# Low parts of two weight chunks in one VectorE operation, in the plain steps of the first w_down stage

## What is computed

```python
h = rms_norm(x, norm_ffn_g[i])
u = causal_dwconv(h @ w_up[i], ffn_conv_w[i])
u_g, u_v = jnp.split(u, 2, axis=-1)
x = x + (jax.nn.silu(u_g) * u_v) @ w_down[i]        # w_down: 5632 x 2048, float32
```

## Time and profile before

| | |
|---|---|
| median of 3 runs | 1567.11 us (1565.79 to 1567.94) |
| the profiled execution, its own time | 1566.66 us |
| its span in the trace | 1564.9 us |
| TensorE (PE) busy | 1558.2 us |
| VectorE (DVE) busy | 1097.1 us |
| ScalarE (ACT) busy | 792.3 us |
| granted clock of TensorE | 1.0 of full speed in all of the stage's windows |

### The profile page before, as it was taken

The page is one execution under the profiler, slowest core; times in us unless marked ns, Lnnn a source line. Parts: engine busy times, 40 slices in busy tenths (PEclk is TensorE's granted clock), DMA queues, the critical chain, the costliest instruction groups (busy, mean ns, idle before and its releaser), DMA issues.

```text
span 1564.9 us, 20899 instructions
## 1 busy us (share of the span) xinstructions
PE 1558.2 (100%) x7694; PEld 1316.9 (84%) x7694; DVE 1097.1 (70%) x1311; ACT 792.3 (51%) x944; POOL 33.7 (2%) x52
## 2 busy tenths in 40 slices
PE   9999999999999999999999999999999999999998
PEld 7878888888888888888888888888888888888887
DVE  6599867766676556555687777789867777755554
ACT  6355454444554544455455555545545555555443
POOL 5000110000000000000000000000000000000000
PEclk9999999999999999999999999999999999999999
DMA  8756665666655666666666566666766666666664
GB/s 260 207 174 189 198 174 168 196 183 188 201 180 174 198 200 195 188 182 180 188 184 194 176 184 203 188 185 204 217 187 187 189 188 175 199 201 188 187 189 149
DMA packets 157479, 297.35 MB, mean 190 GB/s; under 512 B 9655, under 2 KB 14499, under 8 KB 157408
## 3 DMA queue, kind: packets, MB, share of 16 engines
q1 hardware_dynamic: 156896, 296.13, 62.6%
q0 software_dynamic: 480, 0.26, 0.1%
q10 hardware_dynamic: 32, 0.01, 0.0%
HBM read 294.27 MB, written 2.10 MB: 189 GB/s over the span
## 4 chain that ended last, share of the span: by engine, by line
PE 97%; DVE 1%; ACT 0%; DMA 0%; issue 0%; SPq 0%; ACTq 0%
PE psum L541 21%; PE psum L568 18%; PE psum L570 18%; PE psum L569 18%; PE psum L547 11%; PE psum L530 2%; PE psum L532 2%; PE psum L531 2%; PE psum L747 0%; PE psum L693 0%; DVE w_lo L1380 0%; DMA xtok<-in_x 0%; PE psum L668 0%; PE psum L656 0%; PE psum L659 0%
## 5 line engine op out<-in xcount | busy, mean ns | idle before, releaser
L1380 DVE TENSOR_TENSOR w_lo<-raw,w_hi 128x1024 fp32r<-128x1024 f32 x547 | 664.4, 1222 | 379.0 <-ACT w_hi L1019 378.0
L1019 ACT CAST w_hi<-raw 128x1024 fp32r<-128x1024 f32 x546 | 569.7, 1049 | 585.9 <-PE psum L570 391.3
L541 PE MATMUL psum<-h_both,w_hi 128*128 128x512 f32 x1408 | 336.4, 391 | 0.0
L568 PE MATMUL psum<-w_hi,h_both 128*128 128x512 f32 x844 | 331.9, 393 | 0.0
L570 PE MATMUL psum<-w_hi,h_both 128*128 128x512 f32 x844 | 328.7, 389 | 0.0
L569 PE MATMUL psum<-w_lo,h_both 128*128 128x512 f32 x844 | 328.5, 389 | 0.0
L541 PEld LDWEIGHTS psum<-h_both,w_hi 128*128 128x128 f32 x1408 | 258.7, 188 | 50.4 <-DVE rB L1761 0.3
L570 PEld LDWEIGHTS psum<-w_hi,h_both 128*128 128x128 f32 x844 | 158.4, 188 | 33.3
L547 PEld LDWEIGHTS psum<-h_both,w_lo 128*128 128x128 f32 x1408 | 180.6, 191 | 6.9
L568 PEld LDWEIGHTS psum<-w_hi,h_both 128*128 128x128 f32 x844 | 158.5, 188 | 32.7 <-issue 0.3
L569 PEld LDWEIGHTS psum<-w_lo,h_both 128*128 128x128 f32 x844 | 158.6, 188 | 31.8
(11 more groups left out here) (326 smaller groups left out, 1399.0 us busy)
## 6 DMA issues: line engine op xcount, KB each, us to landing
raw<-in_w_up SPq DMA_DIRECT2D x176, 512.0 KB, 3.8
raw<-in_w_gate SPq DMA_DIRECT2D x96, 512.0 KB, 3.6
raw<-in_w_in SPq DMA_DIRECT2D x89, 512.0 KB, 3.7
raw<-in_w_down SPq DMA_DIRECT2D x88, 512.0 KB, 4.3
raw<-in_w_out SPq DMA_DIRECT2D x32, 512.0 KB, 4.1
raw<-in_w_ple_gate SPq DMA_DIRECT2D x32, 512.0 KB, 4.5
raw<-in_w_moba_out SPq DMA_DIRECT2D x16, 512.0 KB, 4.7
raw<-in_w_conv_out SPq DMA_DIRECT2D x8, 512.0 KB, 3.9
```

What stands on the lines that cost most here:

```text
L541: mm = nc.tensor.matmul(wide[part][:, j, :], w_hi[:, c % RING, w], h_both[:, kt + k, :, :].rearrange("p h s -> p (h s)"), start=first and ...
L568: nc.tensor.matmul(o, sh, w_hi[:, c % RING, w], start=first and k == 0, stop=False, skip_group_check=True)
L1019: A.copy(w_hi[:, c % RING, :], raw[:, c % RING, :]).then_inc(chunk_high, 1)
L1380: V.tensor_tensor(w_lo[:, c % RING, :], raw[:, c % RING, :], w_hi[:, c % RING, :].bitcast(F32), ALU.subtract).then_inc(chunk_split, 1)
```

## The change

In a plain step of the first w_down stage the low parts of both chunks are made by one operation over both slots (2 x 1024 columns), once the second chunk's high part is there. It adds 2 to `chunk_split`. Nothing is done any more at the step's first chunk. Chunks of the seven steps and all other stages keep `split`.

```diff
+        def split_pair(c):
+
+            splits[0] = c + 2
+            slots = slice(c % RING, c % RING + 2)
+            dve.wait_ge(chunk_high, c + 2)
+            V.tensor_tensor(w_lo[:, slots, :], raw[:, slots, :], w_hi[:, slots, :].bitcast(F32),
+                            ALU.subtract).then_inc(chunk_split, 2)
...
             g, s, side = place(k)
             c = DOWN1 + k
-            if g > 1 or s not in SEVENS[g]:
+            if g > 1:
                 split(c)
+                return
+            if s not in SEVENS[g]:
+                if side:
+                    split_pair(c - 1)
                 return
```

## The result

| | before | changed |
|---|---|---|
| median of 18 runs each | 1566.57 us | 1569.29 us |
| span of the profiled execution | 1564.9 us | 1567.7 us |
| TensorE busy | 1558.2 us | 1558.3 us |
| VectorE busy | 1097.1 us | 1096.7 us |

The ratio is 1.0018, with a 95% interval of 1.0011 to 1.0024: slower by 2.8 us, between 1.7 and 3.8. The three runs known ahead of the prediction had a median of 1567.11, the 18 have 1566.57.

The account below looks back on a forecast made before the run. TensorE was taken to bound the kernel, through its waits on VectorE. Losses of 1.12 + 1.80 + 0.28 less 0.76 us gave 2.44, hence a median of 1569.6 us, 0.16% slower, counted as the same; range 1566.7 to 1572.2.

Parts of the forecast that it names:

- What bounds the kernel: Whole kernel: TensorE, busy 1558.2 of 1564.9 us, so time moves only with its waits; two old waits cost 0.76 us.
- The operation: VectorE's joint operation of 2048 columns: 2.29 us taken, saving about 1 us over 16 pairs.
- Chunks 0 to 3: First two pairs of the stage: no cost to TensorE, but the scaling of `upv` moves by 1.06 us.
- Chunks 4 and 5: Pair behind VectorE's first tap, delayed through the late scaling: TensorE loses 1.12 us.
- Chunks 6 and 7: Pair behind `full`, with its cast about 1 us late: TensorE loses 1.80 us.
- Chunks 8 and 9: Seven step: VectorE 2.06 us late, TensorE later still, so both old waits go, saving 0.76 us.
- Chunks 10 and 11: Pair behind the first seven step, its casts late: TensorE loses 0.28 us.
- The sum: Whole stage: losses at chunks 4, 6 and 10 less the old waits, 2.44 us slower; given 65%.
- Behind that: From pair 14, 15 on: no further wait, by a margin of 0.45 us, the cycle repeating with later steps.
- Late loads: Rival: later issued loads delay the seven steps' sums, slower by over 0.2%, 1570.3 to 1572.5 us; 21%.
- Nothing is lost: Rival: TensorE finds the pairs ready and old waits shrink, -0.8 to +0.5 us, 1566.3 to 1567.6; 14%.

Follow-up runs that it names:

- the expectation for chunks 12 and up: Joint operations only for chunks 12 and up, single ones before, against the changed kernel; expected -0.2 to +0.3 us, measured stage time 126.43 us, +0.55 against before, ratio 1.0000.
- the kernel with two operations: Changed kernel with the joint operation split into two of 1024 columns, both issued at the step's second chunk; stage time 125.94 us, +0.06 against before, ratio 1.0001.

## Why the prediction was right

*What bounds the kernel.* TensorE's waits alone carried the difference: its busy time is the same within 0.1 us, the sum of its lost time is 2.74 of 2.78 us.

*The operation.* 2.29 us was taken, 2.28 to 2.29 measured for all 16. The saving of about 1 us of VectorE's busy time came out as 0.4; the sum didn't use it.

*Chunks 0 to 3.* The pair 2, 3 was to cost TensorE nothing and to make the scaling 1.06 us late. Measured: no wait there, and the scaling 1.14 later against chunk 0's first matmul (1010.44 - 1006.71 against the end of the old operation at 1009.23 plus 0.03, less 1006.67). The kernel with this pair alone shows that link: +1.13 us.

*Chunks 4 and 5.* Expected 1.12 us lost, measured 1.22. *Chunks 6 and 7.* Expected 1.80, measured 1.94. *Chunks 8 and 9.* No wait expected, none seen; `t_lo` ended at 1034.03, and the first matmul behind its wait started at 1034.37 without idle time. *Chunks 10 and 11.* Expected 0.28, measured 0.34. The sum, 2.44, was 0.3 too small. Much of that is a few hundredths at each link: the joint operation starts 0.10 us behind its cast and not 0.03, and `full` 0.10 behind the second tap's end and not 0.03. That the median of 1569.29 lies within 0.3 us of the 1569.6 foretold is in part luck: the starting value, the median of three runs, was 0.54 too high and the sum 0.3 too low. The change itself, 2.7 to 2.8 us against 2.44, is the fairer comparison.

*Behind that.* No further wait was expected, by a margin of 0.45 at chunk 14, and none was seen. The margin was 0.28: the pair 14, 15 ended at 1046.49, with the 0.2 for coming into step that is 1046.69, and TensorE started chunk 14 at 1046.97. The sums for chunk 12 came 2.49 us later than before, and not 2.06, with their load the last that they waited for. The prediction had written down where this rests, TensorE's own delay. In the expectation for chunks 12 and up I left it out, and missed that waits can come when that delay isn't there.

*Late loads.* This rival is refuted for the changed kernel: its rounds between sums are 1047.10 - 1037.11 = 9.99 and 9.87 us, against 10.25 before and 10.05 in the next round, which the prediction didn't look at, and VectorE's idle time ahead of the sums is 0.49 to 0.61 us, not longer than the 0.60 and 1.10 of before. *Nothing is lost* failed at its first link, the scaling.

*One thing the prediction did not see.* It summed the waits by chunk, and that gave the right total. But the waits aren't separate costs: with the largest taken away, 0.06 of 1.94 us came back. TensorE is released by VectorE at several points, and the total is set by how late VectorE's chain is at the last of them. Counted from chunk 0's first matmul, chunk 8's low part starts 2.28 us later than before in the changed kernel and 2.20 later in the one with single operations for 6 and 7. The rule of the Trainium skill that the prediction weighed (Perfetto Trace Analysis, Optimizing Scalar/DVE Operations: breaking up instructions may let work complete sooner where an engine isn't saturated but makes bubbles on others) is the one that held, on an engine that is 88% busy in the stage: the single operations finish the stage 2.78 us sooner. The share alone didn't decide it. The idle time lay ahead of the second halves, 1.58 us at chunk 3 and 2.12 at chunk 7, and there the first halves' work costs nothing, as the kernel with two operations shows.

## What to carry to other kernels

Joining two operations gives both the later of their two waits. Before doing so, look at the idle time ahead of the second: if the first one fills it, the join moves that work behind the wait, and the 0.06 us that the join saves (2.35 against 2.29) stand against 1.1 us of lateness for everything behind it in the engine's order. And don't take the longest wait of the bounding engine for the cause: ask how late the releasing engine's chain is at each point of release, since the wait that you remove may only come back at the next one. Where runs tell one part in a thousand, the time between two fixed instructions of the bounding engine agreed within 0.05 us for kernels that should not differ; check beside it whether the loads landed alike, since that alone moved a start by 0.3 us.

## What the runs showed of the hardware

A VectorE operation of 2048 columns started 0.10 us behind the end of the cast that it waited for (1008.11 against 1006.96 + 1.05 in the changed kernel), one of 1024 columns 0.03 us (1006.36 against 1005.28 + 1.05 in the kernel with two operations). Writing the operands as one run of 2048 left it at 0.10 (1007.14 against 1005.99 + 1.05), so the shape isn't the reason; whether the length is, or the wait's or the counter's form, stays open. The casts are these rows of ScalarE's time-ordered view, of the changed kernel, the one with two operations and the one with one run of 2048:

```profile
1006.96 1.05 ACT L1019 CAST w_hi<-raw 128x1024 fp32r<-128x1024 f32 x1 [1.75 <-PE psum L541]
```

```profile
1005.28 1.05 ACT L1019 CAST w_hi<-raw 128x1024 fp32r<-128x1024 f32 x1 [1.75 <-PE psum L541]
```

```profile
1005.99 1.05 ACT L1019 CAST w_hi<-raw 128x1024 fp32r<-128x1024 f32 x1 [1.75 <-PE psum L541]
```

And a TensorE wait costs less than its idle time shows: 0.53 us idle cost 0.38, 1.37 cost 1.22, 2.09 cost 1.94 and 0.50 cost 0.34, each about 0.15 less. So a wait is costed by the starts of the matmuls around it, not by the idle time of the weight load.
